# A decoder layer with 32 experts: a new order in the front, from the loads of x to the first expert's rows

## The reference

```python
n = rms_norm(x, norm1_w)
q, k, v, u = split(n @ w_in)                      # 512, 128, 128, 512 columns
q, k = partial_rope(rms_norm(q)), partial_rope(rms_norm(k))
a = sliding_window_attention(q, k, v, sinks)      # window 128, 8 query heads on 2 key heads
p = multiscale_pool(u, pool_w, pool_scale)        # windows 2, 4, 8, 16
h = x + concat(a, p) @ w_out
logits = rms_norm(h, norm2_w) @ w_router + b_router
gates = softmax(top 4 of 32)
y = h + sum over the token's four experts of gate * (act(n2 @ w_gu[e] + b_gu[e]) @ w_down[e] + b_down[e])
```

## Time and profile before

| | |
|---|---|
| median of 3 runs | 1019.15 us (1017.13 to 1019.48) |
| the profiled execution | 1018.11 us, of which the span is 1016.3 us |
| TensorE busy | 956.9 us, 94% of the span |
| VectorE, ScalarE, GpSimd busy | 203.9, 115.8, 16.3 us |
| moved | 418.86 MB, 412 GB/s over the span |
| chain that ended last | TensorE 61%, transfers 34%, VectorE 3%, ScalarE 1% |

### The profile page before, as it was taken

The page is one execution under the profiler, slowest core; times in us unless marked ns, Lnnn a source line. Parts: engine busy times, 40 slices in busy tenths (PEclk is TensorE's granted clock), DMA queues, the critical chain, the costliest instruction groups (busy, mean ns, idle before and its releaser), DMA issues.

```text
span 1016.3 us, 11032 instructions
## 1 busy us (share of the span) xinstructions
PE 956.9 (94%) x4509; PEld 378.3 (37%) x4509; DVE 203.9 (20%) x621; ACT 115.8 (11%) x248; POOL 16.3 (2%) x10
## 2 busy tenths in 40 slices
PE   7999999999998999989899899988999999999987
PEld 4555433333233333333333333323343333333332
DVE  2746211211012111211112111111112111110120
ACT  2431100010001000010001000010001100000001
POOL 0023000000000000000000000000000000000000
PEclk9999999999999999999999999999999999999999
DMA  9996899999999999999999999999999999999994
GB/s 366 399 398 227 317 411 433 428 429 430 432 433 430 432 433 431 432 433 432 432 429 431 431 433 432 432 431 433 432 432 432 408 430 430 430 431 433 429 422 164
DMA packets 20348, 418.86 MB, mean 412 GB/s; under 512 B 2400, under 2 KB 2784, under 8 KB 6144
## 3 DMA queue, kind: packets, MB, share of 16 engines
q1 hardware_dynamic: 19888, 418.12, 96.8%
q10 hardware_dynamic: 432, 0.34, 0.1%
HBM read 417.40 MB, written 1.05 MB: 412 GB/s over the span
## 4 chain that ended last, share of the span: by engine, by line
PE 61%; DMA 34%; DVE 3%; ACT 1%; issue 1%; SPq 0%; DVEq 0%; ACTq 0%
DMA ring<-w_gu_dram 34%; PE ps L1097 30%; PE ps L1185 15%; PE ps L1067 4%; PE ps L1052 4%; PE ps L956 3%; PE ps L894 2%; PE ps L1145 1%; PE ps L1153 1%; ACT PR L513 1%; DMA ring<-w_qkv_dram 0%; PE ps L1222 0%; PE ps L936 0%; DVE PR L701 0%; DVE passing L705 0%
## 5 line engine op out<-in xcount | busy, mean ns | idle before, releaser
L1097 PE MATMUL ps<-ring,passing 128*64 128x512 f32 x1008 | 233.2, 612 | 21.6 <-DMA ring<-w_gu_dram 21.6
L1097 PE MATMUL ps<-ring,PR 128*64 128x512 f32 x1008 | 230.8, 608 | 18.6 <-DMA ring<-w_gu_dram 17.9
L1185 PE MATMUL ps<-ring,PT 128*64 128x512 f32 x988 | 220.5, 599 | 0.5 <-DVE PT L861 0.5
L848 DVE TENSOR_SCALAR tT<-ps 128x256 f32<-128x256 f32 x64 | 27.2, 424 | 670.6 <-PE ps L1097 670.6
L1097 PEld LDWEIGHTS ps<-ring,passing 128*64 128x64 f32 x1008 | 74.9, 141 | 171.5 <-issue 137.2
L1097 PEld LDWEIGHTS ps<-ring,PR 128*64 128x64 f32 x1008 | 73.4, 140 | 167.3 <-issue 136.1
L1185 PEld LDWEIGHTS ps<-ring,PT 128*64 128x64 f32 x988 | 68.7, 137 | 130.8 <-issue 130.1
L574 ACT ACTIVATE tT<-tT 128x256 f32<-128x256 f32 x64 | 26.7, 417 | 492.0 <-DVE tT L848 492.0
L1067 PE MATMUL ps<-PT 64*128 64x512 f32 x256 | 71.7, 639 | 0.8 <-ACT PT L569 0.8
L1052 PEld LDWEIGHTS ps<-qk,N 128*128 128x128 f32 x512 | 59.5, 191 | 20.4 <-issue 20.4
L1052 PE MATMUL ps<-qk,N 128*128 128x128 f32 x512 | 65.4, 281 | 0.8 <-DVE qk L816 0.8
(11 more groups left out here) (162 smaller groups left out, 354.7 us busy)
## 6 DMA issues: line engine op xcount, KB each, us to landing
ring<-w_gu_dram SPq DMA_DIRECT2D x56, 4096.0 KB, 28.7
ring<-w_down_dram SPq DMA_DIRECT2D x28, 4096.0 KB, 29.8
ring<-w_gu_dram SPq DMA_DIRECT2D x6, 2048.0 KB, 10.4
ring<-w_gu_dram SPq DMA_DIRECT2D x4, 3072.0 KB, 24.9
ring<-w_down_dram SPq DMA_DIRECT2D x4, 2048.0 KB, 21.8
ring<-w_mix_dram SPq DMA_DIRECT2D x2, 2048.0 KB, 26.5
ring<-w_gu_dram SPq DMA_DIRECT2D x4, 1024.0 KB, 15.4
ring<-w_down_dram SPq DMA_DIRECT2D x1, 3584.0 KB, 26.4
```

What stands on the lines that cost most here:

```text
L848: nc.vector.tensor_scalar(gb[:, b, :], gu[:, b, 0, :], LIMIT, None, ALU.min).then_inc(g_ready, 1)
L1097: last = mm(ps[64 * j:64 * j + 64, GU + b, :], lhs, halves[j][:, 512 * b:512 * b + 512], start=start, stop=stop)
L1185: last = mm(ps[64 * j:64 * j + 64, bank, :], at[:, k, 64 * (c - GU_PIECES):64 * (c - GU_PIECES) + 64], rows[:, 512 * j:512 * j + 512], sta ...
```

## The change

Names as above. What it does:

- x by feature comes in four parts, with `w1c` in the first; the weights of q, k, v in six parts, ahead of x by token. The constants come in one transfer.
- `project_qkv` takes each of the first six chunks for both tiles, then the last two for tile 0, then for tile 1. More of `project_u` stands ahead of the transposes.
- The pooling's products with tile 0 stand ahead of `transpose_probs(0)`, with one product over 256 columns where there were two of 128. On VectorE `ot_out(0)` stands ahead of `softmax_in(1)`; on ScalarE the scaled copies of the pooling ahead of `softmax_exp(1)`.
- `rsqrt` has one seed instruction and two rounds of four.
- h is transposed into banks 1 and 6 (`HT`). The squares are summed by halves. `open_sums` is four ScalarE copies from X into the banks.
- N2 is x times norm 2's weights on GpSimd for both tiles, without the norm factor; S1 carries the factor instead of ones.
- The triangle carries 1024 on its diagonal, so the ranks come out of one product with the mark of the chosen tokens in them, and one addition makes the table (`rank_of`). Ranks, table, S1 and first gather go tile by tile. The gather's two halves lie in banks 0 and 1.
- An expert's first chunks wait for the first half of `xe` alone. The transposes of the gates for the down bias (`GdT`) move into the first expert, behind its gather, with a wait for their copy.
- Piece 3 waits for the q, k, v projection alone; the buffer with number 4 is issued ahead of the second half of piece 7.

```diff
-    passed = -1.0 - SLOTS * np.repeat(np.arange(PASSES + 1), NE)
-    order = np.concatenate([i[:, None] < i[None, :], np.ones((P, P), bool)], 1)
+    passed = -SELECTED - SLOTS * np.repeat(np.arange(PASSES + 1), NE)
+    order = np.concatenate([(i[:, None] < i[None, :]) + SELECTED * np.eye(P), np.ones((P, P))], 1)
...
+        HT = (1, 6)
...
+        X_CUTS, W_CUTS = ((0, 1), (1, 2), (2, 4), (4, 8)), ((0, 1), (1, 2), (2, 3), (3, 4), (4, 6), (6, 8))
...
             load_qkv(0)
             load_xd(1)
             load_qkv(1)
+            load_xd(2)
             load_qkv(2)
+            load_qkv(3)
+            load_xd(3)
+            load_qkv(4)
+            load_qkv(5)
             sp.dma_start(X[:, :, :], x_tok.rearrange("p (t d) -> p t d", t=T)).then_inc(ld_x, 16)
-            load_qkv(3)
-            load_qkv(4)
+            sp.dma_start(C[:, :], fixed).then_inc(ld_fixed, 16)
...
+            sp.wait_ge(proj, 2)
+            load_piece(3)
             sp.wait_ge(proj, 4)
-            for s in range(3, 5):
-                load_piece(s)
+            load_piece(4)
             load_ahead(0)
...
+            sp.wait_ge(hT_psum, 2)
+            sp.wait_ge(opened, 2)
+            sp.wait_ge(h_ss, 2)
+            sp.wait_ge(weighed, 1)
+            load_ahead(4)
             sp.wait_ge(h_psum, 2 * T)
             load_piece(7, first=PIECE // 2)
             load_ahead(3)
-            sp.wait_ge(opened, 1)
-            sp.wait_ge(h_ss, 1)
-            sp.wait_ge(n2_sb, 1)
-            load_ahead(4)
-            sp.wait_ge(n2_sb, T)
+            sp.wait_ge(weighed, T)
             load_ahead(5)
-            sp.wait_ge(opened, T)
+            sp.wait_ge(hT_psum, 2 * T)
+            sp.wait_ge(opened, 2 * T)
+            sp.wait_ge(h_ss, 2 * T)
             load_ahead(6)
...
-            pool.wait_ge(h_sb, 2 * T)
-            nc.gpsimd.tensor_tensor(N2[:, 1, :], X[:, 1, :], w2b, ALU.mult).then_inc(weighed, 1)
+            for t in range(T):
+                pool.wait_ge(h_sb, 2 * t + 2)
+                nc.gpsimd.tensor_tensor(N2[:, t, :], X[:, t, :], w2b, ALU.mult).then_inc(weighed, 1)
...
-            softmax_exp(1)
             act.wait_ge(mix_psum, 1)
             for g in range(NG):
                 nc.scalar.activation(mixP[:, g, :], ps[:, MIXED[g // 2], 256 * (g % 2):256 * (g % 2) + 256], ACT.Copy,
                                      scale=scl[:, g:g + 1]).then_inc(mix_sb, 1)
+            softmax_exp(1)
             pt_out(1)
             softmax_exp(2)
...
+            def square(t, c):
+                act.wait_ge(h_sb, 2 * t + c + 1)
+                if t > 0:
+                    act.wait_ge(h_ss, 2 * t)
+                nc.scalar.activation(squares[:, c, :], X[:, t, 512 * c:512 * c + 512], ACT.Square, accum_out=h_sq[:, t, c:c + 1]).then_inc(h_ss, 1)
...
+            def open_sums(t):
+                for c in range(2):
+                    nc.scalar.copy(ps[:, ACC[t] + c, :], X[:, t, 512 * c:512 * c + 512]).then_inc(opened, 1)
+            square(0, 0)
+            square(0, 1)
+            hT_out(0)
+            open_sums(0)
+            square(1, 0)
+            hT_out(1)
+            square(1, 1)
+            open_sums(1)
...
-                    nc.scalar.activation(N2[:, 1, :], N2[:, 1, :], ACT.Copy, scale=rms[:, 1:2]).then_inc(n2_sb, 1)
...
+                if step == "first":
+                    act.wait_ge(GdT_psum, 1)
+                    nc.scalar.copy(GdT, ps[0:NE, DWN, 0:T * P].rearrange("p (t s) -> p t s", t=T)).then_inc(GdT_sb, 1)
...
-            def rsqrt(y, v, t):
-                link(nc.vector.tensor_scalar(y.bitcast(I32), v.bitcast(I32), 1, None, ALU.logical_shift_right))
-                link(nc.vector.tensor_scalar(y.bitcast(I32), y.bitcast(I32), -1.0, RSQRT_MAGIC, ALU.mult, ALU.add))
-                for n in range(3):
+            def rsqrt(y, v, t, gain):
+                scale = gain * 9 / 64
+                link(nc.vector.tensor_scalar(y.bitcast(I32), v.bitcast(I32), -0.5, RSQRT_SEED + 2.0**23 * float(np.log2(gain)), ALU.mult, ALU.add))
+                for n in range(2):
                     link(nc.vector.tensor_tensor(t, y, y, ALU.mult))
-                    link(nc.vector.scalar_tensor_tensor(t, t, -0.5, v, ALU.mult, ALU.mult))
-                    last = nc.vector.scalar_tensor_tensor(y, t, 1.5, y, ALU.add, ALU.mult)
-                    if n < 2:
+                    link(nc.vector.scalar_tensor_tensor(t, t, 1.0 / scale**2, v, ALU.mult, ALU.mult))
+                    link(nc.vector.scalar_tensor_tensor(t, t, -10.0 / 3.0, t, ALU.add, ALU.mult))
+                    last = nc.vector.scalar_tensor_tensor(y, t, 5.0, y, ALU.add, ALU.mult)
+                    scale *= 8 / 3
+                    if n == 0:
                         link(last)
                 return last
...
-                nc.vector.tensor_scalar(lm[:, t:t + 1], top[:, t, 0:1], -1.0, None, ALU.mult).then_inc(top_in, 1)
...
+                nc.vector.tensor_scalar(lm[:, t:t + 1], top[:, t, 0:1], -1.0, None, ALU.mult).then_inc(top_in, 1)
...
+            ot_out(0)
             softmax_in(1)
-            ot_out(0)
...
             rms2(0)
-            dve.wait_ge(ld_w2, 16)
-            dve.wait_ge(split, 5)
-            nc.vector.scalar_tensor_tensor(N2[:, 0, :], X[:, 0, :], rms[:, 0:1], w2b, ALU.mult, ALU.mult).then_inc(n2_sb, 1)
             pick(0)
-            weigh(0)
-            h_out(1)
+            def rank_of(t):
+                dve.wait_ge(ranks, t + 1)
+                link(nc.vector.tensor_tensor(rank[:, t, :].rearrange("p (r e) -> p r e", e=NE),
+                                             ps[:, LOGITS, RANKS + t * NE:RANKS + (t + 1) * NE].unsqueeze(1).to_broadcast([P, PASSES + 1, NE]),
+                                             passed.rearrange("p (r e) -> p r e", e=NE), ALU.add))
+            def build_s_of(n, t):
+                for i in range(2):
+                    ins = nc.vector.tensor_scalar(S1[:, t, i * SLOTS:(i + 1) * SLOTS], iota[:, 0:SLOTS], rank[:, t, bass.ds(n + i, 1)],
+                                                  rms[:, t:t + 1], ALU.is_equal, ALU.mult)
+                return ins
+            h_half(1, 0)
+            rank_of(0)
+            build_s_of(0, 0).then_inc(s_first, 1)
+            h_half(1, 1)
             hT_out(1)
             rms2(1)
             pick(1)
-            dve.wait_ge(ranks, 1)
-            link(nc.vector.scalar_tensor_tensor(rk, ps[:, RANKS, 0:T * NE].rearrange("p (t e) -> p t e", t=T), 1.0, sel[:, :, :], ALU.add, ALU.mult))
-            link(nc.vector.tensor_tensor(rank.rearrange("p t (r e) -> p t r e", e=NE),
...
+            rank_of(1)
+            build_s_of(0, 1).then_inc(s_ready, 1)
...
-            build_s(0)
+            link(nc.vector.tensor_reduce(cnt, ps[:, LOGITS, RANKS + T * NE:RANKS + (T + 1) * NE], AX_X, ALU.max))
+            nc.vector.tensor_copy(cnti.bitcast(I32), cnt).then_inc(count_ready, 1)
             build_oneh(0)
...
+            weigh(0)
...
-            project_qkv(0, range(4))
-            project_qkv(1, range(4))
-            project_qkv(0, range(4, KC))
-            project_qkv(1, range(4, KC))
-            pe.wait_ge(ld_id, 16)
+            for k in range(KC - 2):
+                for t in range(T):
+                    project_qkv(t, k)
+            for t in range(T):
+                for k in range(KC - 2, KC):
+                    last = project_qkv(t, k)
+                last.then_inc(proj, 1)
...
-            project_u(0, range(4))
+            project_u(0, range(6))
+            pe.wait_ge(ld_fixed, 16)
             pe.wait_ge(roped, 1)
             transpose_qk(0)
-            project_u(0, range(4, KC))
+            project_u(0, range(6, KC))
             pe.wait_ge(qk_out, 6)
             pe.wait_ge(qkT_sb, 2)
             score(0)
             pe.wait_ge(uv_out, 2)
-            project_u(1, range(2))
+            project_u(1, range(4))
             pe.wait_ge(roped, 2)
             transpose_qk(1)
-            project_u(1, range(2, 4))
+            project_u(1, range(4, 6))
             pe.wait_ge(qkT_sb, 4)
             score(1)
-            project_u(1, range(4, KC))
-            transpose_probs(0)
+            project_u(1, range(6, KC))
+            def pooled_of(g):
+                return ps[:, POOLED[g // 2], SEQ * (g % 2):SEQ * (g % 2) + SEQ]
             pe.wait_ge(ld_bands, 32)
             pe.wait_ge(uv_out, 3)
             for g in range(NG):
-                o = ps[:, POOLED[g // 2], 256 * (g % 2):256 * (g % 2) + SEQ]
-                mm(o[:, 0:P], U[:, 0, g * P:(g + 1) * P], band[:, g, 0:P], start=True, stop=True)
-                mm(o[:, P:SEQ], U[:, 0, g * P:(g + 1) * P], band[:, g, P:SEQ], start=True, stop=False)
-                pe.wait_ge(uv_out, 4)
-                last = mm(o[:, P:SEQ], U[:, 1, g * P:(g + 1) * P], band[:, g, SEQ:SEQ + P], start=False, stop=True)
+                mm(pooled_of(g), U[:, 0, g * P:(g + 1) * P], band[:, g, 0:SEQ], start=g % 2 == 0, stop=False, skip_group_check=True)
```

(72 more changed lines are left out.)

153 lines of the change are left out of this document (65 added, 88 removed).

## The result

The changed kernel takes 1012.69 us (median of 4 runs, 1011.72 to 1013.04), the kernel before 1018.33 beside it (4 runs, 1017.13 to 1019.48): a ratio of 0.994, 95% interval 0.9922 to 0.9959. Run again in twelve executions beside the experiments it took 1015.49 (1011.98 to 1016.14) against 1017.36, a ratio of 0.9967 (0.9953 to 0.998). The ratio on record isn't that of the two medians, which would be 0.9982 here; that of the means is 0.9965. The first profiled execution took 1013.04 us with a span of 1011.2, 5.1 less than before; the profile of the repeat has a span of 1013.6, 2.7 less.

The account below looks back on a forecast made before the run. The weight stream was taken to bound the kernel, gains coming only from its unfed front. First expert 5.2 us earlier, less 0.85 inside it, gave -4.35 us: 1014.6 us, likeliest range 1012.5 to 1016, widened to 1011.5 to 1017.5.

Parts of the forecast that it names:

- What bounds the kernel: Weight stream at 430 GB/s; the end moves one for one with the issue at 129.97, after the first expert's down-projection.
- 1. Start: q, k, v projection: smaller first x part and shared weight chunks end it 0.5 us earlier, bounds 0 and 1.5.
- 2. Norm chain: VectorE's norm and first softmax: tile 0 finishes later, roots are shorter; softmax output 1.2 us later.
- 3. TensorE's order: Attention's middle: pooling ahead of the probabilities' transposes and earlier scaled copies start the output projection 0.9 us earlier.
- 4. Tile 1: Tile 1's residual to gather: earlier copy, shorter root, fewer rank steps; the gather comes 2.45 us earlier, earlier steps included.
- 5. Gather: First gather: tile 0's half done in the choice's wait, -1.9 us; expert waits for the first copy only, -0.85.
- 6. Inside the first expert: TensorE waits for the turned gates' copy ahead of the first expert's transposes: +0.85 us, bounds 0.3 and 1.2.
- Only half arrives: Rival: start gains nothing, new wait costs 1.2, additions and GpSimd contention are dear; -2.7 us, 1016.4; chance 0.14.
- The clock falls at the new waits: Rival: TensorE's pauses at 49 and 95.6 lower its clock once or twice, 1.7 us each; about 1017; chance 0.06.
- The stream is slower: Rival: weight stream behind the front below 430 GB/s, 2.0 us per 1 GB/s; at 425, 1024; chance 0.05.
- More arrives: Case: the start gives 1.5 and the gates' wait costs 0.3; -5.9 us, 1013; chance 0.75 together with the sum.

Follow-up runs that it names:

- all_busy: Changed kernel with both mends, transposes filling the last expert's wait and the pauses around tile 1's ranks, three zero products before the projection: 1011.47 us, ratio 0.9924 to before.
- gates_late: Changed kernel with the gates for the final bias transposed behind the activation's transposes and copied after the other gates: 1013.73 us, ratio 0.9959 to before.
- extra_first: Changed kernel with twelve more transposes of the gates ahead of the first expert's down-projection: 1014.32 us, ratio 0.9973 to before.
- old_order: Changed kernel with the old attention order: probabilities transposed before all pooling, second exponentials before scaled copies, second softmax before attention's copy: 1016.26 us, ratio 0.9974 to before.
- tail_busy: Changed kernel with both mends, plus 16 transposes of the identity in TensorE's wait for the last expert's activation: 1010.25 us, ratio 0.9926 to before.
- both mends: Changed kernel with gates turned behind the activation's transposes and GpSimd's product by halves: 1013.43 us, ratio 0.9959 to before.
- pool_halves: Changed kernel with GpSimd's two products done in halves, each started once its half of h is there: 1013.02 us, ratio 0.9957 to before.

## Why the prediction was right, by its steps

**What bounds the kernel.** Shown. From the issue to the last wait it took 831.70 us before and 831.66 after, with 831.1 to 832.2 in eleven other profiles and 832.66 in all_busy, while the issue itself moved between 123.2 and 129.97.

**1. Start.** The term was mis-sized: 0.5 taken, 1.88 and 0.49 measured in two executions, 0.5 to 2.75 over all ten profiles with this start. What the sum didn't have is the first product's own start, 0.4 to 1.2 earlier (I had counted 0.3, from the x ahead of it alone), and that the length of the projection varies by 1.6 from execution to execution. The bound of 1.5 was too near. The kernel before has one profile only, so how much its own start scatters isn't known. Less of it comes from the change than that: old_start, with the old loads and loops, still has tile 1's copies at 29.63.

**2. Norm chain.** 20.6 us from tile 1's copies to the transposes was forecast, 20.63 measured: two chunks later, two instructions fewer in each root.

**3. TensorE's order.** 6.0 forecast, 6.00 measured, and undoing it gives 8.04. The second softmax is out at 59.7 and asked for at 61.77, a margin of 2.1 (2.3 forecast).

**4. Tile 1.** 6.8 forecast, 7.46 measured: the one term of the sum that was off in both executions. The copy comes 1.44 after the residual (1.3), and the addition and the one-hots took 0.33 and 0.54 (0.35 and 0.44). The step that failed is GpSimd's contention: I held it to the 0.18 of the earlier trace rows, a stretch of one instruction, and it is a wait for GpSimd's end. From copy to gather that made 6.02 instead of 5.5, and with the product by halves it is 5.49. The row of before shows it too, read with the earlier trace rows: 94.36 and 0.34 is 94.70, and 92.33 and 2.35 is 94.68. The Trainium skill (GPSIMD Engine Reference, Specifications) names the shared interface; by the rule I had weighed 0.7 us, and the extra over a step's 0.16 was 0.52 here.

**5. Gather.** 2.01 from gather to first expert, 1.9 forecast; the old 4.69 is gone.

**6. Inside the first expert.** +0.74 for a forecast of +0.85 (the forecast's own times, 122.15 and 121.25, would give 0.90), and 0.73 back when the gates are turned elsewhere.

**The rivals.** *Only half arrives*: in the repeat the span fell by 2.7, but neither for a start that gives nothing nor for a dearer wait; of the 1.65 that it fell short, 1.18 lies behind the last wait, where the clock fell and which I had held fixed, and 0.64 in tile 1. *The clock falls at the new waits*: it did in 3 of 13 profiles (gates_late, extra_first, old_order), at the price given, about 1.6 us; not in the two of the changed kernel. 0.06 was too low for a single execution. Whether it moves a median wasn't shown. *The stream is slower*: no, 430 and 430 GB/s. *More arrives*: its start came in one of the two executions, its shorter wait for the gates didn't. What I hadn't weighed at all is that the stretch behind the last wait isn't fixed: 52.7 to 56.1 us over the fourteen profiles.

## What to carry to other kernels

Where a stream bounds the time, look for the last release that finds it dry: here all that lies ahead of it counted one for one up to the last wait for weights, and 1.4 us spent after it cost nothing. The parts of a reordering can depend on one another, here the gather by tile on the seeding by ScalarE, so judge them together and not one by one. When two executions of one kernel differ by 2.4 us, a part worth 0.7 is read from stretches of the profile and not from medians. The best versions found are tail_busy, the change with both mends and a filled last wait, with 1010.25 us, and all_busy, which can't be told from it. Their intervals lie below that of the repeat, and only in part below that of the first measurement; how much the filled wait has in this is open.

## What the runs showed of the hardware that I had not expected

- A VectorE instruction with two inputs in SBUF and one element per partition stood until GpSimd's running instruction was over: 2.14, 0.68, 1.04 and 1.19 us for 0.16, each to within 0.02 us of GpSimd's end where that end has a row. Two instructions of 128x64 with one tensor input took 1.35 instead of 0.54 beside GpSimd's half, at 89.13 in pool_halves; the first of them took 1.13 and so ended at 90.26, where GpSimd's half ended at 90.21.
- The granted clock after pauses of 1 to 3 us isn't the same from execution to execution. Around the first gather (98 to 102 us) it was 1.00 in ten of the 13 profiles with the change and 0.57 to 0.71 in three. Behind the last wait for weights, mostly of 2.6 us, 28 passes took 6.23 us in ten of all 14 profiles and 7.64 to 7.93 in four. Behind the last expert's open wait of 2.19 us, 32 passes took 8.69 to 8.79 in eight of twelve profiles and 7.09 in four. The time from the last wait for weights to the end follows from the last two: 52.7 to 53.2 us with neither fall, 54.5 to 54.8 with one, 55.8 and 56.1 with both. Filled with transposes, the wait of 2.19 us cost no clock in either of two profiles, too few to show that it is the filling.
- A load of 64 KB on a second queue beside the first chunks goes with a first product at 6.02 (one profile) instead of 4.80 to 5.64 us. Why that start scatters by 0.8 us without it stays open.
